# Layer norm between two decoder layers: plain centring of the rows, weights and bias applied on the turned copy, rows finished later

## What is computed

```python
for layer in range(2):
    x = layer_norm(ALPHA * x + token_mixer(x, w_in, ...), ln1_g, ln1_b)
    x = layer_norm(ALPHA * x + moe(x, w_router, ...), ln2_g, ln2_b)

def layer_norm(x, g, b):                   # over the 1024 columns
    mu, var = mean(x), mean((x - mu) ** 2)
    return (x - mu) * rsqrt(var + 1e-5) * g + b
```

## Time and profile before

| what | value |
| --- | --- |
| median of 3 runs | 1231.92 us (1230.57 to 1231.96) |
| profiled execution, device time | 1230.97 us |
| its span, first to last instruction | 1229.2 us |
| granted TensorE clock, mean | 0.997 |
| busy: PE, DVE, ACT, POOL | 98%, 46%, 28%, 10% |
| handover between the layers | about 607.8 to 622.9 us |
| attention stage of layer 1 | about 623 to 751 us |
| experts of layer 1 | about 767 to 1218 us |

### The profile page before, as it was taken

One profiled execution on the slowest core, in us unless ns is written; L12 is line 12 of the kernel. 1 busy time (PEld: TensorE's weight loads), 2 busy tenths in 40 slices (PEclk: granted clock), 3 DMA queues, 4 the chain that ended last, 5 costly groups with the idle time before them and its releaser, 6 DMA issues.

```text
span 1229.2 us, 25333 instructions
## 1 busy us (share of the span) xinstructions
PE 1203.9 (98%) x10419; PEld 626.5 (51%) x10421; DVE 559.7 (46%) x1554; ACT 345.4 (28%) x709; POOL 125.4 (10%) x173
## 2 busy tenths in 40 slices
PE   9999999999999999999999999999999999999996
PEld 8886843344344443433398868344334444443341
DVE  6888653333333333333378877433333333333334
ACT  5667411111111111111266673111111111111111
POOL 2662200000000000000035431000000000000000
PEclk9999999999999999999999999999999999999998
DMA  9554899999999999999945529999999999999994
GB/s 363 188 183 183 326 412 424 426 427 426 427 425 424 428 426 428 425 425 427 387 159 196 223 104 406 407 426 425 425 428 426 425 425 425 427 426 426 425 427 190
DMA packets 42425, 454.88 MB, mean 370 GB/s; under 512 B 4944, under 2 KB 5712, under 8 KB 8016
## 3 DMA queue, kind: packets, MB, share of 16 engines
q1 hardware_dynamic: 42032, 452.27, 88.5%
q10 hardware_dynamic: 288, 1.05, 0.2%
HBM read 452.26 MB, written 1.05 MB: 369 GB/s over the span
## 4 chain that ended last, share of the span: by engine, by line
PE 79%; DVE 11%; DMA 6%; ACT 2%; issue 2%; DVEq 0%; ACTq 0%
PE banks L1100 34%; PE banks L1127 17%; PE banks L1073 7%; PE banks L1138 5%; DMA expert_weights<-in_moe_w 5%; PE banks L1113 2%; PE banks L1017 1%; DVE prob L1753 1%; PE banks L964 1%; ACT prob L1362 1%; PE banks L1054 1%; PE banks L966 1%; DVE sm_neg L1736 1%; PE banks L965 1%; PE banks L661 1%
## 5 line engine op out<-in xcount | busy, mean ns | idle before, releaser
L1100 PE MATMUL banks<-expert_weights,gathered 128*64 128x512 f32 x1520 | 340.3, 595 | 1.4 <-DMA expert_weights<-in_moe_w 1.4
L1100 PEld LDWEIGHTS banks<-expert_weights,gathered 128*64 128x64 f32 x1520 | 105.3, 137 | 229.6 <-issue 229.6
L1127 PE MATMUL banks<-expert_weights,hT 128*32 128x512 f32 x1600 | 182.0, 595 | 2.4 <-DVE gathered L1941 2.3
L1956 DVE TENSOR_TENSOR sig<-sig,banks 128x256 f32<-128x256 f32 (+1 forms) x66 | 27.3, 413 | 339.9 <-ACT sig L1479 339.9
L1492 ACT ACTIVATE y_hi<-banks,gate_slot 128x512 fp32r<-128x512 f32 x126 | 86.6, 687 | 289.7 <-PE banks L1127 289.7
L1966 DVE SCALAR_TENSOR_TENSOR y_lo<-banks,gate_slot,y_hi 128x512 fp32r<-128x512 f32 x126 | 94.6, 751 | 160.4 <-ACT y_hi L1492 160.4
L1479 ACT ACTIVATE sig<-banks 128x256 f32<-128x256 f32 x64 | 24.6, 384 | 409.0 <-PE banks L1100 409.0
L1073 PEld LDWEIGHTS banks<-hot,x_part 128*128 128x128 bf16 x3072 | 93.3, 98 | 50.3 <-issue 50.3
L1127 PEld LDWEIGHTS banks<-expert_weights,hT 128*32 128x32 f32 x1600 | 47.7, 109 | 108.9 <-issue 108.1
L1073 PE MATMUL banks<-hot,x_part 128*128 128x64 bf16 x3072 | 100.7, 193 | 0.0
L1552 POOL TENSOR_TENSOR piece_lo<-pieces,piece_hi 128x256 fp32r<-128x256 f32 x112 | 88.8, 828 | 74.4 <-ACT piece_hi L1301 61.0
(11 more groups left out here) (258 smaller groups left out, 1525.4 us busy)
## 6 DMA issues: line engine op xcount, KB each, us to landing
expert_weights<-in_moe_w SPq DMA_DIRECT2D x132, 2048.0 KB, 23.7
expert_weights_in_ring<-in_moe_w SPq DMA_DIRECT2D x20, 2048.0 KB, 23.8
pieces<-in_pieces SPq DMA_DIRECT2D x32, 1024.0 KB, 6.0
expert_weights<-in_moe_w SPq DMA_DIRECT2D x26, 1024.0 KB, 9.3
expert_weights_in_rows<-in_moe_w SPq DMA_DIRECT2D x22, 1024.0 KB, 22.9
expert_weights_in_x<-in_moe_w SPq DMA_DIRECT2D x22, 1024.0 KB, 23.6
expert_weights_in_ring<-in_moe_w SPq DMA_DIRECT2D x8, 1024.0 KB, 9.7
shared_weights<-in_ws SPq DMA_DIRECT2D x2, 3072.0 KB, 12.2
```

The lines of the kernel that those rows point to most:

```text
L1100: mm = pe.matmul(C[e * PAIR:(e + 1) * PAIR, :], xgT[:, d, e * PAIR:(e + 1) * PAIR], w[e][:, part], start=(d == 0), stop=(d == KD - 1))
L1127: mm = pe.matmul((A, B)[c][to:to + SLOTS, :], hT[:, f, of_:of_ + SLOTS], W[QUARTERS + c][e][:, f * 512:(f + 1) * 512], start=(f == 0), sto ...
```

## The change

The rows of x are centred and divided only (one `tensor_scalar` out of PSUM for each half, written to `x_sb`). TensorE turns these. ScalarE's copy out of PSUM applies weight and bias, which on the turned side are one value per partition, so that each block k of 128 columns takes an instruction of its own: 8 for a tile, where there were 2 copies. TensorE waits for each block alone. The rows get weight and bias later on VectorE, after `rotate(1)`, by two `tensor_tensor` of 128x1024 for each tile. A small new DMA brings the turned weights. ScalarE waits for the rows before it writes into `rtmp`. The dummy matmuls between the two turns of tile 0 are gone. In the first expert step `read_gathered` now stands ahead of `read_hT`.

```diff
 SyncE, after the last expert weights of a layer
                     sp.dma_start(lnp[:, :, :]..., of(lnw)[0, 1].partition_broadcast(P)).then_inc(ln_ld, 16)
+                    sp.dma_start(ln_cols[:, :, :], of(ln_t)[0]).then_inc(ln_ld, 16)
 TensorE
-                    def project_first(t, g):
-                        for k in range(4 * g, 4 * g + 4):
+                    def project_first(t, ks):
+                        for k in ks:
...
-                        turn_first(0)
-                        keep_clock(3)
-                        turn_second(0)
...
-                        turn_first(1)
-                        turn_second(1)
-                        for g in range(2):
-                            pe.wait_ge(*at(xt_sb, 7 + g, 1))
-                            project_first(1, g)
+                        def turn_centred(t):
+                            for g in range(2):
+                                pe.wait_ge(*at(ln_first, 2 * t + g + 1, 1))
+                                turn_x_half(pe, t, g, bank[4 + 2 * t + g])
...
+                        for t in range(TT):
+                            turn_centred(t)
+                            for k in range(KD):
+                                if t == 0 and k % 4 == 0:
+                                    pe.wait_ge(*at(first_piece[k // 4], 16))
+                                pe.wait_ge(*at(xt_sb, 2 * TT + t * KD + k + 1, 1))
+                                project_first(t, (k,))
 ScalarE
+                    def columns_out(t):
+                        for k in range(KD):
+                            if k % 4 == 0:
+                                act.wait_ge(*at(xt_ps, 4 + 2 * t + k // 4 + 1, 1))
+                            act.activation(xT[:, k, t * P:(t + 1) * P], bank[4 + 2 * t + k // 4][:, k % 4 * P:(k % 4 + 1) * P], ACT.Identity,
+                                           scale=ln_cols[:, 0, k:k + 1], bias=ln_cols[:, 1, k:k + 1]).then_inc(xt_sb, 1)
...
+                        act.wait_ge(*at(ln_ld, 48, 1))
                         deviation(3, (0,), 1)
                         split_hi(1)
-                        copy_xT(act, 4, 0, (bank[4], bank[5]), 1)
+                        columns_out(0)
                         deviation(4, (1,), 1)
                         split_hi(2)
-                        copy_xT(act, 4, 1, (bank[6], bank[7]), 1)
+                        columns_out(1)
...
                     split_hi(6)
+                    if layer:
+                        normalised(act, 1, TT - 1, 1)
 VectorE
+                    def rows_out(t):
+                        dve.wait_ge(*at(ln_ld, 48, 1))
+                        dve.wait_ge(*at(xt_ps, 4 + 2 * t + 2, 1))
+                        own.link(V.tensor_tensor(x_sb[:, t, :], x_sb[:, t, :], lnp[:, 0, :], ALU.mult))
+                        V.tensor_tensor(x_sb[:, t, :], x_sb[:, t, :], lnp[:, 1, :], ALU.add).then_inc(ln_done, 1)
...
                     rotate(1)
+                    if layer:
+                        for t in range(TT):
+                            rows_out(t)
...
-                        if first:
-                            read_hT(main, n + 1)
                         if not last:
                             read_gathered(main, 1 - s, n + 2)
                         if not last:
+                            read_hT(main, n + 1)
                             if not first:
-                                read_hT(main, n + 1)
                                 dve.wait_ge(*at(main.sc, n))
...
-                            deviations(1, (t,), halves[0])
-                            stretch(t, halves[0], ln_first)
-                            centre(1, t, halves[1])
-                            stretch(t, halves[1])
+                            deviations(1, (t,), late=True)
+                            own.settle()
+                            for c in range(2):
+                                cols = slice(c * 512, (c + 1) * 512)
+                                V.tensor_scalar(x_sb[:, t, cols], bank[2 * t + c], ln_s[:, t, 12:13], ln_s[:, t, 18:19], ALU.subtract, ALU.mult).then_inc(ln_first, 1)
```

More of the change, by code:

```diff
@@ L132, in restart, with build @@
         self.n = 0
-def build(nc, x, x_t, first, pieces, rows, small, moe_w, ws, router, lnw, consts, out):
+def build(nc, x, x_t, first, pieces, rows, small, moe_w, ws, router, lnw, ln_t, consts, out):
     ctx = ExitStack()
@@ L873, in _ @@
                             for t in range(TT):
-                                project_first(t, g)
+                                project_first(t, range(4 * g, 4 * g + 4))
                     else:
[L876 to L884, removed]
+                        def turn_centred(t):
+                            for g in range(2):
+                                pe.wait_ge(*at(ln_first, 2 * t + g + 1, 1))
+                                turn_x_half(pe, t, g, bank[4 + 2 * t + g])
                         pe.wait_ge(*at(ln_var, TT + 1, 1))
                         keep_clock(4)
-                        turn_first(0)
-                        keep_clock(3)
-                        turn_second(0)
-                        for g in range(2):
[L892 to L896, removed]
-                        turn_first(1)
-                        turn_second(1)
-                        for g in range(2):
-                            pe.wait_ge(*at(xt_sb, 7 + g, 1))
-                            project_first(1, g)
+                        for t in range(TT):
[5 more added lines that the diff above has]
+                                project_first(t, (k,))
                     project_by_terms(1)
@@ L1541, in _ @@
                     else:
-                        for t in range(TT):
-                            normalised(pool, 1, t, 1)
+                        pool.wait_ge(*at(ln_first, 2 * TT, 1))
                     for t in range(TT):
@@ L1841, in centre @@
                     def centre(second, t, cols):
-                        dve.wait_ge(*at(ln_ld, 16 * (second + 1)))
+                        dve.wait_ge(*at(ln_ld, 16 + 32 * second))
                         xx = x_sb[:, t, cols]
@@ L1852, in _, with deviations @@
                     whole, halves = slice(0, D), (slice(0, 512), slice(512, D))
-                    def deviations(second, tiles, cols=whole):
+                    def deviations(second, tiles, cols=whole, late=False):
                         own.settle()
@@ L1861, in deviations @@
                         V.tensor_scalar(v, ln_s[:, tiles[0]:tiles[-1] + 1, 13], LN_EPS, None, ALU.add).then_inc(ln_var, 1)
-                        centre(second, tiles[0], cols)
+                        if not late:
+                            centre(second, tiles[0], cols)
                         dve.wait_ge(*at(ln_rs, second * TT + tiles[-1] + 1))
```

13 lines of the change are left out of this document (7 added, 6 removed).

## The result

| | median us (executions) | ratio to before, 95% interval |
| --- | --- | --- |
| before | 1231.94 (8) | |
| changed kernel | 1234.59 (8, 1233.52 to 1237.25) | 1.0026 [1.0016, 1.0036] |

The change costs 2.65 us in the median, 2.0 to 4.4 us by the interval, so it is slower, and just over the 2.5 us (0.2%) that I had named as the limit of what can be told from no change. The forecast was 1233.4 with a range of 1230.2 to 1235.7.

What follows compares the result with a forecast made beforehand. TensorE held 79% of the chain of waits, with experts' stages ending when their weights land. First exp +1.9 us, less 0.4 for the expert steps, gave +1.5 on 1231.92: 1233.4 us, range 1230.2 to 1235.7.

Steps and rivals of the forecast that it cites:

- The columns and the root: ScalarE at the handover: 0.345 us per column block, eight in 2.76, delaying tile 1's square root from 615.43 to 615.78.
- The second half of a tile: VectorE's normalising at the handover: 0.70 us with a step of 0.66, second half in time for its columns.
- x_hi and the terms: Handover: x_hi starts at 621.40 instead of 620.30, TensorE's three-term products 0.5 us later; TensorE's delay put at 0.6.
- The rows: VectorE after rotate(1): four operations of 4.8 us plus 1.7 waiting for GpSimd, 6.5 in all, linked ones waiting longer.
- What sets the first exp: Attention's start in layer 1: VectorE 2.3 to 2.4 us late, less 0.45 slack, makes the first exp 1.9 late.
- The first expert step: Swapped reads let TensorE's down start up to 0.42 us earlier; gain taken as 0.2 per layer, 0.4 together.
- GpSimd, the DMA, ScalarE's new wait: TensorE's wait for GpSimd's piece 4, the turned-weights DMA and ScalarE's wait for the rows: each costed at nothing.
- my own case: The prediction's main account, columns and rows delaying the first exp: 1232.2 to 1234.6 us, chance 0.44.
- the rival in which the rows wait 0.75 each: Rows fight GpSimd all the way, columns cost 0.39 us, first exp 3.7 late: 1235.4 us; chance 0.22.
- The rival that attention absorbs the delay: Attention has hidden slack, VectorE's 1.9 us counts nothing and expert steps give 0.4: 1231.5 us; chance 0.12.
- that of cheap columns and hidden rows: Blocks at 0.25 us, rows 4.8 without waiting for GpSimd, TensorE's products 0.9 early: 1230.4 us; chance 0.22.

Runs made afterwards that it cites:

- e5: Changed kernel with ScalarE taking tile 1's square root between column blocks 3 and 4 of tile 0: 1232.67 us, ratio 1.0004.
- e11: Changed kernel with ScalarE's 16 column blocks as plain copies, leaving layer 1's turned x without weight and bias: 1232.03 us, ratio 1.0006.
- e3: The changed kernel once more, unaltered, on the same chip as other follow-up runs: 1233.83 us, ratio 1.0024.
- e6: Changed kernel with the four rows operations moved behind VectorE's \|z\| instead of ahead of it: 1233.61 us, ratio 1.0016.
- e4: Changed kernel without the four rows operations, so layer 1's rows stay without weight and bias: 1233.17 us, ratio 1.0017.
- e1: Kernel before with only read_gathered put ahead of read_hT in the first expert step of both layers: 1231.25 us, ratio 0.9996.
- e9: Kernel before with only the small DMA of turned weights and the wait counts for it, its data unread: 1231.77 us, ratio 0.9999.
- e7: Changed kernel with the square root early, the rows behind \|z\|, and x_hi and x_lo made for each tile: 1233.42 us, ratio 1.0013.
- e10: Changed kernel with early root, rows behind \|z\|, x_hi and x_lo by tile, and the old first-expert-step order: 1232.41 us, ratio 1.0009.
- e8: Changed kernel with GpSimd's rests of piece 4 held back until the rows are finished: 1238.51 us, one execution.

## Why the prediction came out as it did

- **The columns and the root.** Predicted 0.345 us a block, measured (2.89 - 0.46) / 7 = 0.347, where a single block lasts 0.46. By the Trainium skill, page "ScalarE: Activation LUTs", section "What ACT_TABLE_LOAD costs", I had estimated 0.386; the trace does not agree, the blocks overlap by some 0.11 us, more than the 93 ns it gives. The root had no idle time before it, as predicted, and was late by 0.23 us (predicted 0.35). e5 and e11 show both links of this step.
- **The second half of a tile.** Predicted at 0.70 us with a step of 0.66; the pair took 1.53, 0.8 each with a step of 0.7. The second half was nevertheless in time for the fifth block.
- **x_hi and the terms.** `x_hi` +0.85 (predicted +1.10), TensorE's terms +0.43 (+0.5) with 0.69 idle behind `x_hi`, its first product of piece 4 +0.81 (+0.6): 647.61 - 612.40 against 642.15 - 607.75.
- **The rows.** 6.50 us with the contention of 1.62 (predicted 6.5 and 1.7). The split between linked and other instructions was wrong: the first two took 1.46 and 1.65, the last two 1.76 and 1.65, and the two linked ones (1.46 and 1.76) are not the slower ones. Each of them loses about 0.4 as long as GpSimd runs.
- **What sets the first exp.** |z| +2.33 (predicted 2.3), the first exp +1.97 (+1.9; +2.12 in e3). The size was right, and the path that I followed is the one in the changed kernel's trace: `split_lo(6)` waits there for `split_hi(6)`, behind the exp of |z|. In my list of VectorE's idle times, 1.47 and 1.73 us, the 3.67 ahead of the gates were missing. It did no harm, because I counted ScalarE's slack at |z| instead, nearly the same time seen from the other engine. The idle time between `rotate(1)` and `split_lo(6)` was 1.47 + 3.67 + 1.73 = 6.87, more than the rows' 6.5, and still they cost time. The sum comes out in the trace: VectorE ends `rotate(1)` 1.01 us late, spends 6.64 on the rows with their link, fills 6.87 - 1.57 = 5.30 of idle time, and starts `split_lo(6)` 1.01 + 6.64 - 5.30 = 2.35 late (+40.70 for +38.35). The 1.57 stay idle because `split_hi(6)` stands behind the late |z|, and e6 shows that moving the rows past it opens a gap of 1.26 elsewhere. The second path to the exp, by TensorE and the weights, I did not see; it would have given 0.9 by itself (e4).
- **The first expert step**, "0.2 each, 0.4 together": the term for which no run shows anything at the end. The 0.2 was near the truth at `down`, which won 0.17 us of wait in layer 1; the bound of 0.42, the length of one copy, was too high, as the order only swaps two copies that are both needed. That 0.4 would reach the end was an assumption; the profiles' stretch from the exp to the end shows none of it, and e1's ratio of 0.9996 [0.9987, 1.0005] can neither show nor exclude it.
- **GpSimd, the DMA, ScalarE's new wait**: nothing, as costed. e9 shows it for the DMA. TensorE did not wait for piece 4, and ScalarE not for the rows. The granted clock stayed at 1.00 through the changed kernel's handover without the dummy matmuls.

By the trace the sum is +1.97 to +2.1 at the exp and +1.65 to +2.3 at the end of the span, against +1.5 predicted; leaving out the expert step's 0.4 closes most of that. The rest of the measured 2.65 lies inside the interval, whose lower end is 1.0016, 2.0 us; the forecast's +1.5 lies below that end.

The time of 1234.59 is at the upper edge of my own case (1232.2 to 1234.6) and above 1234.4, a region to which I had given 0.26, mostly for the rival in which the rows wait 0.75 each. They waited 0.4 each, so the mechanism is that of my case and not of that rival. The rival that attention absorbs the delay is out, and so is that of cheap columns and hidden rows: a block costs 0.347 us and the rows are not hidden. In one point the +1.9 for the exp had luck: the path by the weights was left out, and it did not count because it ended 1.05 us ahead of VectorE's.

**What stays open.** e7's timed runs lie 0.5 to 2.8 us above before by their interval, while its marks are level and its end 0.8 us early. e10, the same but for the order, is compatible with nothing (0.9999 to 1.0018). The DMA is excluded by e9 to within 0.0008, the order by e1 to within 0.0005, in the kernel before. Whether something small remains outside the handover, or the profiled execution of e7 was a lucky one, these runs don't tell. One candidate is visible: falls of the clock ahead of the tail stand in the profiles of the changed kernel, e5 and e6 (0.81 and 0.85 near 85 us) and e8, each worth one or two us, and in no other; but they stand at places that have nothing to do with the handover in three of the four, and one profile of each kernel says little on how often they come. The landing of the last weights of layer 0 varies by up to three us from execution to execution, and one profile holds one draw of each.

No version ran faster than the kernel before. Of those that keep the new scheme and compute everything, e5 (1.0004) and e10 (1.0009) can't be told from it in the timed runs; by their marks e7 and e10 are level with it, and e5 is 1.4 us behind at the first exp.

## What to carry to other kernels

Work taken off the busiest engine of a stage is worth only what the next engine in the loop leaves of it: here a per-partition scale and bias nearly doubled the time of ScalarE's copies (1.49 to 2.89 us for eight), and a tiny instruction queued behind them, the square root, gave back the time that VectorE had won. When work is put into an engine's idle time, list every gap up to the next point where another engine waits for it; here one of 3.67 us was overlooked, and moving the work past one visible wait (e6) only opened another. Ask also which other path ends at the same point: taking work off one shows the next one. And compare single profiled executions from a mark close to the edit, since here everything ahead of it varied by more than the effect.

## What the runs showed of the hardware that was not expected

- VectorE's `tensor_tensor` with both inputs in SBUF takes 1.22 us for 128x1024 with GpSimd idle and 1.65 to 1.76 beside it. GpSimd's 128x256 take 0.75 us each alone. In the changed kernel it has done 2.83 / 0.75 = 3.8 of its eight when the rows begin at 640.00, and needs 7.09 us for the other 4.2, an estimate of 1.7 us each; its timeline over 640.5 to 643 shows two that took 3.40 together. That is the time of one of VectorE's. Both readings fit two engines taking turns, one instruction for one, at the cost mostly of the engine with the shorter ones; I had expected 1.35.
- Column blocks with a scale and a bias start every 0.347 us; plain ones of 0.27 us start every (1.49 - 0.27) / 7 = 0.17. So the two pointers cost about 0.175 us of each block also where blocks overlap.
- After a wait of 2.5 us TensorE's clock fell in two profiles (the changed kernel and e5: a mean of 0.69 over 600 to 605 us, between the levels of 2.4 and 1.2 GHz; 16 products in 5.35 and 5.18 us) and not in a third (e9: 3.65 us). In e8 it fell to 0.83 over 645 to 655 us, around its wait of 2.73. Behind waits of up to 1.99 us at that place (e1) it stayed at 1.00.
